# Moving a 31-tap depthwise convolution from VectorE to TensorE column strips in a fused transformer kernel

## What is computed

```
def conformer_conv_mixer(x, w_pw1, b_pw1, w_dw, b_dw, ln_g, ln_b, w_pw2, b_pw2):
    h = x @ w_pw1 + b_pw1                       # [256, 2048]
    a, gate = jnp.split(h, 2, axis=-1)
    h = a * jax.nn.sigmoid(gate)                # GLU, [256, 1024]
    h = causal_depthwise_conv(h, w_dw) + b_dw   # 31 taps for each channel
    hf = h.astype(F32)
    mean = jnp.mean(hf, axis=-1, keepdims=True)
    var = jnp.mean(jnp.square(hf - mean), axis=-1, keepdims=True)
    hf = (hf - mean) * lax.rsqrt(var + LN_EPS) * ln_g + ln_b
    return jax.nn.silu(hf) @ w_pw2 + b_pw2
```

## Time and profile before

| what | value |
|---|---|
| median of three runs | 2137.82 us (2137.1 to 2138.12) |
| the profiled execution, its own time | 2135.27 us |
| its span | 2133.5 us |
| PE, DVE, ACT, POOL busy, share of the span | 94%, 62%, 46%, 4% |
| mean granted TensorE clock | 0.967 |
| PE busy in the Conformer's stretch 1122.50 to 1240.80 us | 72.85 us of 118.30 |
| DVE busy in the same stretch | 99.99 us |
| chain of waits over the whole span, by engine | PE 83%, DVE 9%, ACT 5%, issue 2%, DMA 1% |

### The profile page before, as it was taken

How to read it: one execution, slowest core, us unless ns; L and a number is a source line. 1 busy time by engine, 2 the same in 40 slices (tenths; PEclk the granted TensorE clock), 3 DMA queues, 4 the chain that set the end, 5 groups by cost and what they waited for, 6 DMA issues and landing times.

```text
span 2133.5 us, 25642 instructions
## 1 busy us (share of the span) xinstructions
PE 1995.6 (94%) x10412; PEld 1691.7 (79%) x10412; DVE 1323.9 (62%) x1721; ACT 972.9 (46%) x1265; POOL 77.7 (4%) x109
## 2 busy tenths in 40 slices
PE   4999999999999999999997589999999999999998
PEld 3778888877888787788877468888888888778887
DVE  4755665665655674566568946566675567556654
ACT  4544444553544534454447044445354453345443
POOL 0310000030000000000000000000000000000000
PEclk9989999989999999999998789999999999999999
DMA  5602665521665564456644117654556556535661
GB/s 200 203 9 89 207 196 179 174 81 40 207 191 185 188 196 151 140 171 195 192 134 140 68 40 227 192 187 164 182 183 188 187 181 205 170 121 170 196 197 61
DMA packets 196093, 340.58 MB, mean 160 GB/s; under 512 B 5701, under 2 KB 127177, under 8 KB 195976
## 3 DMA queue, kind: packets, MB, share of 16 engines
q1 hardware_dynamic: 193316, 331.27, 47.9%
q10 hardware_dynamic: 2660, 7.67, 1.0%
HBM read 337.87 MB, written 1.05 MB: 159 GB/s over the span
## 4 chain that ended last, share of the span: by engine, by line
PE 83%; DVE 9%; ACT 5%; issue 2%; DMA 1%; POOL 0%; SPq 0%; DVEq 0%; ACTq 0%
PE ps L472 18%; PE ps L474 17%; PE ps L473 17%; PE ps L580 13%; PE ps L578 7%; DVE arena L1656 3%; DVE w_lo L1312 2%; PE ps L577 2%; ACT w_hi L883 2%; PE ps L731 1%; PE ps L716 1%; PE ps L724 1%; ACT xT L924 1%; PE ps L723 1%; DMA w_raw<-w_in_dram 1%
## 5 line engine op out<-in xcount | busy, mean ns | idle before, releaser
L1312 DVE TENSOR_TENSOR w_lo<-w_raw,w_hi 128x2048 fp32r<-128x2048 f32 x316 | 723.1, 2293 | 285.0 <-ACT w_hi L883 284.4
L883 ACT ACTIVATE w_hi<-w_raw 128x2048 fp32r<-128x2048 f32 x316 | 601.3, 1913 | 142.0 <-PE ps L474 120.9
L472 PE MATMUL ps<-w_hi,u_h 128*128 128x512 f32 (+1 forms) x1056 | 418.0, 396 | 9.8 <-DVE u_l L1632 3.0
L580 PE MATMUL ps<-xT,w_hi 128*128 128x512 f32 x1176 | 419.2, 396 | 0.0
L474 PE MATMUL ps<-w_hi,u_l 128*128 128x512 f32 (+1 forms) x1056 | 413.1, 391 | 0.0
L473 PE MATMUL ps<-w_lo,u_h 128*128 128x512 f32 (+1 forms) x1056 | 412.9, 391 | 0.0
L578 PE MATMUL ps<-xT,w_lo 128*128 128x256 f32 x1344 | 347.3, 279 | 0.0
L472 PE MATMUL ps<-w_hi,xT 128*128 128x512 f32 (+2 forms) x800 | 287.9, 360 | 17.2 <-DVE xT L1370 17.2
L474 PE MATMUL ps<-w_hi,xT 128*128 128x512 f32 (+2 forms) x800 | 284.0, 355 | 0.0
L473 PE MATMUL ps<-w_lo,xT 128*128 128x512 f32 (+2 forms) x800 | 283.9, 355 | 0.0
L578 PEld LDWEIGHTS ps<-xT,w_lo 128*128 128x128 f32 x1344 | 253.4, 189 | 13.6
(11 more groups left out here) (190 smaller groups left out, 1892.1 us busy)
## 6 DMA issues: line engine op xcount, KB each, us to landing
w_raw<-mlp_w_dram SPq DMA_DIRECT2D x128, 1024.0 KB, 5.4
w_raw<-ret_w_in_dram SPq DMA_DIRECT2D x48, 1024.0 KB, 5.1
w_raw<-w_up_dram SPq DMA_DIRECT2D x32, 1024.0 KB, 5.5
w_raw<-w_down_dram SPq DMA_DIRECT2D x32, 1024.0 KB, 4.9
w_raw<-w_in_dram SPq DMA_DIRECT2D x16, 1024.0 KB, 5.6
w_raw<-ret_w_out_dram SPq DMA_DIRECT2D x16, 1024.0 KB, 4.9
w_raw<-cf_w_pw_dram SPq DMA_DIRECT2D x12, 1024.0 KB, 5.2
w_raw<-sc_w_in_dram SPq DMA_DIRECT2D x12, 1024.0 KB, 5.1
```

Source lines behind the costliest of these rows:

```text
L472: pe.matmul(dst, lh, rh, start=start, stop=False)
L580: ins = pe.matmul(ps[:, bank, :], w_hi[:, slot, wsl], both, start=False, stop=kc == KC - 1)
L883: act.activation(w_hi[:, slot, :], w_raw[:, slot, :], ACT.Copy).then_inc(hi_ready[slot], 1)
L1312: tt(w_lo[:, slot, :], w_raw[:, slot, :], w_hi[:, slot, :].bitcast(F32), ALU.subtract).then_inc(lo_ready[slot], 1)
```

## The change

All 8 chunks are convolved on TensorE. The 31 taps are padded to 32 and split as k = 4r + t. For each chunk the four groups g of 32 channels are copied four times into a ring of three buffers, `z4`, the copy of partitions 32t to 32t+31 shifted by t tokens: 16 DMAs of [32 x 284] for each chunk, issued on SP (`shifted`). Then 8 sets r x 4 groups g are float32 matmuls with 128 rows (4 taps x 32 channels), 32 output columns and 256 tokens; group g writes PSUM partitions 32g to 32g+31, so the four groups use four column strips of the array. ACT adds the bias on the way out. The weights `tap_w` are built once, during the MLP ahead: POOL sorts the taps, ACT issues 16 DMAs of [32 x 64] that move them to the right partitions, and POOL multiplies them into masks (4 products of 128 x 2048). The diagonal weights and all of `convolve` go. The statistics are taken half by half: the first four chunks are transposed early, and each token half has its own signal to POOL, DVE and ACT. `uadd` and `ulow` of all MLPs share memory with `relu` and `usq`.

```
-CONV_VEC, CONV_PE = (0, 1, 2, 3, 4, 5), (6, 7)
+Z_RING, Z_LEN, TAP_SETS = 3, 284, 8
...
 SP
+            def shifted(sec, c):
+                sp.wait_ge(glu_done.sem, glu_done.at(sec, c // 2 + 1))
+                if c >= Z_RING:
+                    sp.wait_ge(conv_e.sem, conv_e.at(sec, c - Z_RING + 1))
+                for t in range(4):
+                    for g in range(4):
+                        sp.dma_start(z4[32 * t:32 * t + 32, c % Z_RING, g, :],
+                                     cz[32 * g:32 * g + 32, c, t:t + Z_LEN]).then_inc(z_in[c % Z_RING], 16)
             for sec in sections:
                 for c, view in enumerate(tiles_of(sec)):
                     load(sec, c, view)
+                    if sec.kind == "cf" and c in (5, 7, 9, 11):
+                        shifted(sec, c - 5)
+                        shifted(sec, c - 4)
...
 TensorE, cf
+                def conv(c):
+                    if c == 0:
+                        pe.wait_ge(taps_ready, 1)
+                    if c >= 4:
+                        pe.wait_ge(conv_a.sem, conv_a.at(sec, c - 3))
+                    pe.wait_ge(z_in[c % Z_RING], 256 * (c // Z_RING + 1))
+                    for r in range(TAP_SETS):
+                        for g in range(4):
+                            ins = pe.matmul(ps[32 * g:32 * g + 32, c % 4, 0:S], tap_w[:, g, c, r, :],
+                                            z4[:, c % Z_RING, g, 4 * r:4 * r + S], start=r == 0, stop=r == TAP_SETS - 1)
+                    ins.then_inc(conv_e.sem, 1)
+                up(sec, 6, 2, lambda: turn_ups(sec, 1, cwide, lambda: pe.wait_ge(wu_sb.sem, wu_sb.at(sec, 2))))
+                conv(0)
+                conv(1)
+                up(sec, 7, 3)
+                pe.wait_ge(glu_done.sem, glu_done.at(sec, 1))
+                up(sec, 4, 4)
+                conv(2)
+                conv(3)
+                up(sec, 5, 5)
+                pe.wait_ge(glu_done.sem, glu_done.at(sec, 2))
+                up(sec, 6, 6)
+                up(sec, 7, 7)
+                conv(4)
+                conv(5)
                 pe.wait_ge(glu_done.sem, glu_done.at(sec, 4))
-                for n, c in enumerate(CONV_PE):
-                    pe.wait_ge(diag_ready.sem, diag_ready.at(sec, n + 1))
-                    for k in range(CFK):
-                        ins = pe.matmul(ps[:, n, 0:S], cdiag(CFK * n + k), cz[:, c, k:k + S], start=k == 0, stop=k == CFK - 1)
-                    ins.then_inc(conv_e.sem, 1)
-                pe.wait_ge(conv_v.sem, conv_v.at(sec, 1))
...
+                pe.wait_ge(conv_a.sem, conv_a.at(sec, 4))
+                for t in range(NT):
+                    for c in range(4):
+                        ins = back(c, t)
                 ins.then_inc(conv_T.sem, 1)
+                conv(6)
+                conv(7)
+                pe.wait_ge(conv_a.sem, conv_a.at(sec, KC))
+                for t in range(NT):
+                    for c in range(4, KC):
+                        ins = back(c, t)
+                    ins.then_inc(conv_T.sem, 1)
...
 ACT, mlp
                 begin(prev, sec)
+                if before_cf(sec):
+                    act.wait_ge(taps_sorted, 1)
+                    for t in range(4):
+                        for g in range(4):
+                            act.dma_start(tap_col[32 * t:32 * t + 32, g, :],
+                                          tap_rows[32 * g:32 * g + 32, t, :, :].rearrange("p c r -> p (c r)")).then_inc(taps_in, 16)
                 for t in range(NT):
...
 POOL, mlp
+                step.link(pool.tensor_copy(tap_rows, gcol[:, :, w:w + 32].rearrange("p c (r t) -> p t c r", t=4)))
+                pool.memset(tap_rows[:, 3, :, TAP_SETS - 1], 0.0).then_inc(taps_sorted, 1)
...
+                pool.wait_ge(taps_in, 256)
+                for g in range(4):
+                    ins = pool.tensor_tensor(tap_w[:, g, :, :, :].rearrange("p c r m -> p (c r) m"), tap_mask.unsqueeze(1).to_broadcast(shape),
+                                             tap_col[:, g, :].unsqueeze(2).to_broadcast(shape), ALU.mult)
+                ins.then_inc(taps_ready, 1)
...
 DVE, cf
-                for c in CONV_VEC[2:]:
-                    convolve(c)
                 vec.wait_ge(conv_T.sem, conv_T.at(sec, 1))
+                for t in range(NT):
+                    vec.bn_stats(bns[:, 2 * t, :], ps[:, 4 + 2 * t, :])
+                for t in range(NT):
+                    vec.wait_ge(conv_T.sem, conv_T.at(sec, t + 2))
+                    step.link(vec.bn_stats(bns[:, 2 * t + 1, :], ps[:, 5 + 2 * t, :]))
+                    vec.bn_aggr(mv[:, t, :], bns[:, 2 * t:2 * t + 2, :].rearrange("p a b -> p (a b)")).then_inc(gn_var.sem, 1)
```

More of the change, by code:

```diff
@@ L159, in build @@
         pos_i = sb("pos_i", [P, NT], I32)
+        z4 = sb("z4", [P, Z_RING, 4, Z_LEN])
         ps = ctx.enter_context(nc.psum_tensor("ps", [P, 8, 512], F32))
@@ L191, in build @@
         usq = region(3072, 2, 512)
-        uadd = region(4096, 2, 512)
-        ulow = region(5120, 2, 512)
+        uadd = relu
+        ulow = usq
         rqk = region(0, NT, 2048)
@@ L205, in build @@
         xn = region(0, NT, D)
[L206 to L219, removed]
+        ccv = region(0, KC, S)
+        cz = region(2048, KC, CFK - 1 + S + 2)
+        tap_rows = region(4352, 4, KC, TAP_SETS)
+        tap_w = arena[:, 4608:4608 + 4 * KC * TAP_SETS * 32].rearrange("p (g c r m) -> p g c r m", g=4, c=KC, r=TAP_SETS)
+        tap_col = region(12800, 4, KC * TAP_SETS)
+        tap_mask, tap_half = region(13056, 32), region(13088, 32)
+        csg = region(12800, 2, 2, S)
+        cwide, swide = region(15360, 2, 512), region(7168, 2, 512)
+        ch = region(4608, NT, D)
+        csl = region(6656, 2, 2, S)
+        cbias = region(7680, D)
+        chh = region(8704, NT, D)
         sgb, sgc = region(2048, 2, 2, S), region(3072, 2, 2, S)
@@ L308, in build @@
         glu_done = Stage(sem("glu_done"), {"cf": 4})
[L309 to L313, removed]
+        taps_sorted, taps_in, taps_ready = sem("taps_sorted"), sem("taps_in"), sem("taps_ready")
+        z_in = [sem(f"z_in{i}") for i in range(Z_RING)]
+        conv_e = Stage(sem("conv_e"), {"cf": KC})
+        conv_a = Stage(sem("conv_a"), {"cf": KC})
+        conv_T = Stage(sem("conv_T"), {"cf": 3})
         silu_done = Stage(sem("silu_done"), {"cf": 4})
@@ L342, in up_bank, with before_cf @@
             return 6 - 2 * (k % 2)
+        def before_cf(sec):
+            return sec.index + 1 < len(sections) and sections[sec.index + 1].kind == "cf"
         def two(v):
@@ new lines, in back @@
+                def back(c, t):
+                    return pe.transpose(ps[:, 4 + 2 * t + c // 4, (c % 4) * P:(c % 4 + 1) * P], ccv[:, c, t * P:(t + 1) * P], ident[:])
+                up(sec, 6, 2, lambda: turn_ups(sec, 1, cwide, lambda: pe.wait_ge(wu_sb.sem, wu_sb.at(sec, 2))))
[6 more added lines that the diff above has]
+                conv(3)
@@ L1116, in cf, with conv_out @@
             def cf(prev, sec):
+                def conv_out(c):
+                    act.wait_ge(conv_e.sem, conv_e.at(sec, c + 1))
+                    act.activation(ccv[:, c, :], ps[:, c % 4, 0:S], ACT.Identity, bias=gain("bdw", 0, c)).then_inc(conv_a.sem, 1)
                 begin(prev, sec)
@@ L1137, in cf @@
                     ins.then_inc(sig_ready.sem, 1)
-                    n_diag = len(CONV_PE) * CFK
-                    for d in range(j * n_diag // 4, (j + 1) * n_diag // 4):
-                        ins = act.activation(cdiag(d), ident[:], ACT.Copy, scale=gain("wdw", d % CFK, CONV_PE[d // CFK]))
-                        if d % CFK == CFK - 1:
-                            ins.then_inc(diag_ready.sem, 1)
+                    if j in (1, 2):
+                        conv_out(2 * j - 2)
+                        conv_out(2 * j - 1)
                 prepare(sec, 8)
-                for n, c in enumerate(CONV_PE):
-                    act.wait_ge(conv_e.sem, conv_e.at(sec, n + 1))
-                    act.activation(ccv[:, c, :], ps[:, n, 0:S], ACT.Identity, bias=gain("bdw", 0, c)).then_inc(conv_a.sem, 1)
+                for c in range(4, KC):
+                    conv_out(c)
                 act.dma_start(cbias, a["cf_b_pw2_2"].to_broadcast([P, D])).then_inc(bias_in.sem, 16)
-                act.wait_ge(gn_shift.sem, gn_shift.at(sec, 1))
                 for t in range(NT):
+                    act.wait_ge(gn_shift.sem, gn_shift.at(sec, t + 1))
                     act.activation(two(ch[:, t, :]), ps[:, 4 + 2 * t:6 + 2 * t, :], ACT.Identity, scale=grs[:, t:t + 1],
```

76 lines of the change are left out of this document (21 added, 55 removed).

## The result

The changed kernel takes **2181.52 us** (median of 4 runs, 2180.34 to 2182.51) against 2137.46 before, measured beside it (2135.80 to 2138.12): ratio 1.0206, 95% interval 1.0191 to 1.0221. It is 44 us slower. The forecast was 2145.7 with a range up to 2166, so the direction was the likeliest one and the size was missed by 36 us. Its profiled execution took 2180.34 us, with a span of 2178.5 (before 2133.5).

What follows compares the result with a forecast made beforehand. TensorE sets the pace except in the Conformer's stretch, bound by DVE's convolution. Terms -1.9 + 4.7 + 2.0 + 2.6 + 0.5 = +7.9 us on 2135.27 give 2143.2; the median, 2.5 higher, gives 2145.7 us, range 2119 to 2166.

Steps and rivals of the forecast that it cites:

- A small DMA on SP takes 0.25 us and the next starts 0.3 us later; I take 0.29.: Conformer, SP's copies: 0.29 us per issue, 4.7 us for a chunk's 16, plus 2.0 us to land.
- I take the middle, 0.853 us a round.: TensorE's convolution: strips overlap two records abreast, 0.853 us a round, 6.8 us a chunk, 54.6 us in all; chance 0.53.
- the first rival: Convolution: four strips truly side by side, 0.43 to 0.55 us a round, copy issue paces the stage, 2127 us; chance 0.32.
- faster from about 0.65 us a round: Convolution: the price of a round of four strips from which the first rival decides for a faster kernel.
- ACT 4.7 us later: MLP ahead: 16 tap DMAs at 0.33 us each delay ACT's first relu by 4.7 us, without cover.
- POOL beside DVE, 2.6: MLP ahead: POOL's first tap product holds up DVE's w_lo and u_l of tile 4; 2.6 us, between 0 and 5.1.
- Tap copy, 0.5: MLP ahead: the tap copy of 256 elements beside the last residual update costs 0.5 us, between 0 and 1.5.
- Clock, 2.0: MLP ahead: TensorE's 6.2 us gap before the first relu's product costs 2.0 us of clock.
- The stretch gains 1.9.: Conformer up to the first down matmul: ends at 1238.9 against 1240.84, a gain of 1.9 us.
- The tail: Conformer, end of convolution to first down matmul: 9.8 us instead of 13.9, with half the transposes and statistics done early.
- The fourth GLU held behind tile 10: Conformer: ACT and DVE reach the fourth GLU only after tile 10, loaded after 32 SP issues; it ends at 1204.
- the three marks: New profile: wrong if spacing is under 0.08 or over 0.15 us, copy issue far from 0.29 us, or relu not late.

Runs made afterwards that it cites:

- run 7: Changed kernel with four copies a chunk, weight loads ahead of copies, four tap DMAs in MLP steps 3 to 6, convolution pairs one up step later: 2092.01 us.
- run 6: Changed kernel with one of POOL's four tap products, so three of four channel groups convolve with what lies in memory: 2173.73 us.
- run 5: Changed kernel with ACT's 16 tap DMAs moved from ahead of the first relu to steps 3 to 10 of the same MLP: 2163.93 us.
- run 2: Changed kernel with SP's copies of each pair moved behind three more weight loads: 2175.97 us.
- run 9: Kernel of run 7 with the 32 matmuls of a chunk ordered strip by strip: 2153.18 us.

## Why the prediction was wrong

**"A small DMA on SP takes 0.25 us and the next starts 0.3 us later; I take 0.29."** This step failed, and it made most of the error. The rows I took it from the earlier trace rows are loads of small tensors from HBM. A copy from on-chip memory to on-chip memory costs its queue 0.64 to 0.68 us, on SP and on ACT alike. The trace of before has no such DMA, and I put one number where two bounds were due. With the measured price my own steps do give the new pace. A GLU ends; the second chunk's copies land 2 x 10.2 + 1.3 us later; its convolution takes 6.6 behind the gap, the up step 5.8, sigmoid and GLU 1.9. That is 36.0 us, and the blocks of SP begin 1181.93 - 1145.79 = 36.1 us apart. I had 28.1.

**"I take the middle, 0.853 us a round."** This failed as well, to the good side: 0.42 to 0.45 us, the first rival's price. Both reasons for the middle fell. The 0.11 us of the earlier trace rows was the spacing of some small transposes and no floor of the engine. And the argument that a strip's second record holds back the next strip's first one is refuted by the fours: one record on each strip starts within 0.020 us, and the second ones follow 0.215 us later. So the records of different strips do not start in the order that I took for the program's. The 2.38 times that the Trainium skill reports for three column tiles ("TensorE: Matmul & The Clock Gate", Part 3), scaled to four strips, would give 0.54 us a round, an estimate from its figure. The measurement differs from that, and from the order rule of the same part as I had applied it. "TensorEngine Tiling (Array Packing)", "Theoretical Speedup", allows four, and the trace agrees: 0.445 us a round in run 7, where one strip alone needs 0.427 for each of the four.

**The first rival** had the right mechanism: issue paces the stage and TensorE waits. It gave 2127 because its issue price was the same wrong 0.29. So the forecast's direction was luck: it said slower because of dear strips, which were cheap. With the right price of the strips alone, my steps said 11 us faster. It came out slower because the second error, the DMA's price, was the larger one. The point that I named ("faster from about 0.65 us a round") held for that price only. At 0.64 us a DMA the copies bind at any price of the strips below the issue time of a chunk, 10.2 us, and this rival should have been worked out for a dear DMA too.

**"ACT 4.7 us later"**: the term is right and was mis-sized by the same factor. The sixteen DMAs took 10.3 us, and TensorE's wait grew by 9.8. **POOL beside DVE, 2.6**: the mechanism was right and the place too; products 2 to 4 alone cost 4.9 us with the clock that they took (run 6). That the first product holds up a two-element operation, L1464, for 3 us I had not thought of. **Tap copy, 0.5**: the residual update beside it took 1.72 us, before 1.42: 0.3 longer. In run 5 it takes 1.71 too and the stretch loses nothing, so the term is nothing on the path. **Clock, 2.0**: TensorE's busy time for the same 986 records of the stretch rose from 184.3 to 188.7 us, at a mean granted clock of 0.96 instead of 1.00. That is 4.3 us, of which 1.9 go with products 2 to 4 (186.8 in run 6). Together +9.8 was forecast and +16.7 measured, 12.4 of it idle and 4.3 busy time.

**"The stretch gains 1.9."** It lost 25.8, mainly by 19.9 more waiting for the convolution's inputs and 13.2 more convolving, less 4.5 in the tail. The 13.2 come from the clock. Eight chunks at the price of run 7 are 28.5 us, less than the 29.5 of before; behind their waits they took 42.7. I had 4.5 us for that, and it was 14.2.

**What came out right.** The tail, 9.8 forecast and 9.4 measured. The fourth GLU held behind tile 10, worth 5.5 us by run 2. The order in which things are late: copies, then TensorE, then the GLU. Of the three marks that I had named for being wrong, two came true and named the two steps that failed (spacing under 0.08, a copy's issue far from 0.29). The third did not: the relu was late, and by twice what I had said.

**What stays open.** Why a DMA from on-chip memory costs its queue 0.64 us, and 0.49 from HBM with the same rows. Why a DMA costs more than that in places: in run 7, beside weight loads, SP's blocks of eight took 5.1 to 6.7 us, up to 0.83 us each. Whether copies from two queues would have done as well.

## What to carry to other kernels

Before layout copies go on a queue, count the DMAs, not the bytes: here each cost 0.64 us of the queue that issues it, and 128 of them outweighed 63 us taken off DVE, while the same bytes in 32 made the kernel faster. Put the issues where no engine's next work stands behind them, and order the consumer so that copies run beside other matmuls; a wait of 5 to 10 us on TensorE is followed by a stretch at half the clock: here 52.3 us of waits cost another 14.2 us of convolving. And where matmuls go to separate column strips, interleave the strips in the program.

## What the runs showed of the hardware

- A DMA from on-chip to on-chip memory took its queue 0.64 us on SP (0.68 with the blocks back to back) and 0.65 on ACT, for 32 rows of 256 bytes, 32 rows of 1136 bytes, and 128 rows of 1136 bytes alike; in run 7, beside weight loads, up to 0.83 on SP. With an HBM source and the same 32 rows it was 0.49 (one run); a row load beside it 0.33.
- Four column strips of two-record float32 matmuls overlap fully if interleaved: one record on each strip every 0.215 us, 0.052 us a record against 0.213 in one strip. Strip by strip it is 0.170, since only the last four records of a strip run beside the first four of the next (run 9).
- A two-element DVE operation of 0.16 us took 3.01 us beside a POOL product and ended with it (run 6: 952.31 and 952.29). The Trainium skill ("SBUF — State Buffer", "Who interferes with whom") names single-input operations of this kind (tensor_scalar) among those that can take the shared port; the trace agrees. The prediction had counted only the two-input ones.
- POOL's products 2 to 4 cost 4.9 us at the start of the MLP; all four cost nothing that shows in its middle (run 5: the stretch is as long as before), although every step there has remainders on DVE too. In the steps of the middle DVE stands idle for 1.1 to 1.5 us ahead of several operations (run 5); at the start its operations stand back to back (the kernel before, from 935.70 on for 12 us).
